# Gate tiles of three head pairs as seven block products, in a float32 encoder step on one core

## What is computed

```python
u = rmsnorm(x, norm_w) @ w_in
cq = rmsnorm(u[..., :Q_LORA_RANK], q_norm_w)
gate = u[..., Q_LORA_RANK:]
q = (cq @ w_uq).reshape(B, T, MLA_HEADS, QK_NOPE_DIM + QK_ROPE_DIM)
q_nope = q[..., :QK_NOPE_DIM]
q_pe = rope(q[..., QK_NOPE_DIM:], q_pos)
q_lat = jnp.einsum('bthn,rhn->bthr', q_nope, kv_w_uk)
o_lat = mla_attend(q_lat, q_pe, q_pos, c_kv, k_pe, k_pos)
o = jnp.einsum('bthr,rhv->bthv', o_lat, kv_w_uv).reshape(B, T, MLA_GATE_WIDTH)
return x + (o * jax.nn.silu(gate)) @ w_out
```

## Time and profile before

| | us |
|---|---|
| median of 3 runs | 1047.45 (1046.79 to 1049.26) |
| the profiled execution's own time | 1046.36 |
| its span | 1044.6 |
| TensorE busy | 1019.8 (98%) |
| VectorE busy | 503.3 (48%) |
| ScalarE busy | 259.6 (25%) |
| GpSimd busy | 271.1 (26%) |

### The profile page before, as it was taken

One profiled execution on the slowest core, in us unless ns is written; L12 is line 12 of the kernel. 1 busy time (PEld: TensorE's weight loads), 2 busy tenths in 40 slices (PEclk: granted clock), 3 DMA queues, 4 the chain that ended last, 5 costly groups with the idle time before them and its releaser, 6 DMA issues.

```text
span 1044.6 us, 12018 instructions
## 1 busy us (share of the span) xinstructions
PE 1019.8 (98%) x4334; PEld 654.8 (63%) x4334; DVE 503.3 (48%) x1134; ACT 259.6 (25%) x541; POOL 271.1 (26%) x345
## 2 busy tenths in 40 slices
PE   7999999999989999999999999999999999999998
PEld 4777777777755453444535777777766666655665
DVE  5964444444466566685665532244233333344224
ACT  3222121212154242232431000011222323243221
POOL 3552525252313234142132063311110101010110
PEclk9999999999999999999999999999999999999999
DMA  7224232423375989979798322112210111203202
GB/s 269 78 99 157 92 109 112 156 90 110 111 298 179 397 323 346 373 302 391 300 374 332 146 81 81 55 46 104 92 64 20 63 41 44 88 31 127 79 27 101
DMA packets 44464, 164.20 MB, mean 157 GB/s; under 512 B 4916, under 2 KB 8248, under 8 KB 35456
## 3 DMA queue, kind: packets, MB, share of 16 engines
q1 hardware_dynamic: 44416, 163.56, 42.5%
HBM read 106.32 MB, written 57.23 MB: 157 GB/s over the span
## 4 chain that ended last, share of the span: by engine, by line
PE 63%; DVE 4%; DMA 1%; POOL 1%; ACT 1%; issue 1%; SPq 0%; POOLq 0%; ACTq 0%
PE work_b L708 11%; PE work_a L708 7%; PE work_b L1246 5%; PE work_a L1037 5%; PE bank L1121 5%; PE work_a L936 3%; PE bank L1004 2%; PE work_b L1121 2%; PE work_b L989 2%; DVE arena L2149 2%; PE bank L1291 2%; PE work_a L1316 2%; PE work_a L1276 1%; PE bank L1425 1%; PE work_a L1121 1%; PE work_a L1013 1%
## 5 line engine op out<-in xcount | busy, mean ns | idle before, releaser
L2149 DVE SCALAR_TENSOR_TENSOR arena<-arena,bank 128x512 f32<-128x512 f32 x128 | 87.0, 742 | 59.3 <-PE bank L1004 59.3
L708 PE MATMUL work_b<-arena,ring 128*128 128x320 f32 x384 | 107.8, 433 | 0.0
L708 PEld LDWEIGHTS work_b<-arena,ring 128*128 128x128 f32 x384 | 71.5, 190 | 27.7
L1037 PE MATMUL work_a<-arena 128*128 128x512 f32 x128 | 64.1, 613 | 2.7 <-ACT arena L1581 2.7
L813 PE MATMUL work_a<-arena 128*128 128x320 f32 x224 | 64.9, 433 | 0.4 <-DVE arena L1916 0.4
L813 PE MATMUL work_a<-arena,ring 128*128 128x320 f32 x224 | 64.9, 432 | 0.0
L813 PE MATMUL work_b<-arena 128*128 128x320 f32 x224 | 62.7, 432 | 0.0
L708 PE MATMUL work_a<-arena,ring 128*128 128x320 f32 x192 | 55.4, 449 | 7.2 <-DMA ring<-in_stream 7.2
L2659 POOL COPY arena<-arena 32x640 f32<-32x640 f32 x20 | 16.6, 832 | 163.0 <-ACT arena L1696 156.7
L813 PEld LDWEIGHTS work_b<-arena 128*128 128x128 f32 x224 | 42.6, 190 | 17.7
L708 PEld LDWEIGHTS work_a<-arena,ring 128*128 128x128 f32 x192 | 37.9, 198 | 23.2 <-DMA ring<-in_stream 7.2
(11 more groups left out here) (336 smaller groups left out, 1795.0 us busy)
## 6 DMA issues: line engine op xcount, KB each, us to landing
ring<-in_stream SPq DMA_DIRECT2D x66, 512.0 KB, 3.4
arena<-in_c SPq DMA_DIRECT2D x32, 1024.0 KB, 9.3
out_s_c<-arena SPq DMA_DIRECT2D x32, 1024.0 KB, 6.1
arena<-in_keys SPq DMA_DIRECT2D x8, 664.0 KB, 4.2
v_scratch<-arena SPq DMA_DIRECT2D x16, 320.0 KB, 4.3
k_scratch<-arena SPq DMA_DIRECT2D x16, 320.0 KB, 4.6
z_scratch<-arena SPq DMA_DIRECT2D x16, 320.0 KB, 4.3
arena<-k_scratch SPq DMA_DIRECT2D x4, 1280.0 KB, 13.0
```

What stands on the lines that cost most here:

```text
L708: done = mm(halves(buf)[:, a, :], lhs, rhs[:, a * HALF:(a + 1) * HALF], start=first, stop=last)
L1037: last = mm(pair_bank[q % 2], kh[:, q, t, :], vh[:, :, t, :], start=t == 0, stop=t == NP - 1)
L2149: op = v.scalar_tensor_tensor(ct[s % CS][:, g, :], ct[s % CS][:, g, :], decb[:, h, b:b + 1], bank[g][:, :], ALU.mult, ALU.add)
```

## The change

The two gate tiles that pairs 0 to 2 prepare are formed together. Their product is taken as 2x2 blocks: rows = the two gate tiles, columns = the left and right 320 tokens, inner dimension = input tiles 0 to 3 (upper) and 4 to 7 (lower). Seven products of four matmuls each (320 columns) replace eight such products. For this
- GpSimd forms four combinations of the tokens (4 tiles x 320 = 1280 columns) once, before pair 0 (`mix_gate_tokens`), and four combinations of the weights (4 blocks x 128 = 512 columns) in each of pairs 0 to 2, after `swap_halves` (`mix_gate_weights`);
- TensorE's `gate_products` issues the products in an order in which two accumulate onto earlier ones in PSUM; the filler portions are 8, 6, 4, 6, 2, 2 matmuls, counted in matmuls now and not in blocks;
- ScalarE's `keep_gate` copies two halves of 320 columns instead of two tiles of 640, after the exponentials of blocks 0 and 1;
- VectorE adds five times 320 columns: `gate_sums` after the probabilities of blocks 0, 2 and 3 (one, one, two), `last_gate_sum` after the pair's outputs;
- SyncE reloads both slots of the ring once all seven products of the pair are through; before, each as its tile was through.

```diff
@@ buffers of the attention stage
+        gate_w_mix = [take(KH, P) for _ in range(2)]
+        gate_u4 = take(HALF)
...
+        spare = [osT.rearrange("p a b c d -> p (a b c d)"), lsq.rearrange("p a b -> p (a b)")]
+        gate_x_mix = [shaped(part[:, 0:KH * HALF], (KH, HALF)) for part in (*spare, keys_c, arena[:, root_at:root_at + 2 * T])]
+        gate_w_mix += [shaped(part[:, KH * HALF:KH * HALF + KH * P], (KH, P)) for part in spare]
+        gate_p1, gate_u2 = rstd[:, 0:HALF], rstd[:, HALF:T]
...
+        GATE_MM, GATE_OUT, GATE_KEPT = 7, 5, 2
+        KEPT_E, MIXED_E = NI - 2 + OUT_PAIRS - 1, MIXED_A + 4 * (OUT_PAIRS - 1)
+        X_MIXED = MIXED_E + 4
@@ SyncE
+                sp.wait_ge(gate_mm, GATE_MM * (p + 1))
                 for r in range(2):
-                    load_weight(at + 8 + 2 * p + r, (2 * p + r) % SLOTS, gate_mm)
+                    load_weight(at + 8 + 2 * p + r, (2 * p + r) % SLOTS, None)
@@ TensorE, stage_e
-                def gate_tiles(k_all):
-
-                    for at in k_all:
-                        r, k = divmod(at, KD)
-                        slot = (2 * p + r) % SLOTS
-                        if k == 0:
-                            pe.wait_ge(w_in[slot], c.next(w_in[slot], step=16))
-                            if r == 0:
-                                pe.wait_ge(E.free[1], c.all(E.free[1]))
-                            else:
-                                pe.wait_ge(gate_out, c.all(gate_out))
-                        last = tokens(work[1], ring[:, slot, k, :], xb[:, k, :], k == 0, k == KD - 1)
-                        if k == KD - 1:
-                            last.then_inc(gate_mm, c.up(gate_mm))
-                            c.skip(gate_out)
-
-                gates = iter(range(2 * KD))
+                def gate_products():
+
+                    s0, s1 = 2 * p % SLOTS, (2 * p + 1) % SLOTS
+                    left, right = slice(0, HALF), slice(HALF, T)
+                    low, high = quarter[2], quarter[3]
+                    out, kept, mixed = GATE_OUT * p, KEPT_E + GATE_KEPT * p, X_MIXED + 4 * p
+
+                    def product(dst, weights, tokens_of, fresh):
+                        for k in range(KH):
+                            last = mm(dst, weights[:, k, :], tokens_of[:, k, :], start=fresh and k == 0, stop=k == KH - 1,
+                                      skip_group_check=True)
+                            if k == KH - 1:
+                                last.then_inc(gate_mm, 1)
+                            yield
+
+                    pe.wait_ge(w_in[s0], c.next(w_in[s0], step=16))
+                    pe.wait_ge(E.free[1], c.all(E.free[1]))
+                    yield from product(low, ring[:, s0, upper, :], xb[:, upper, left], True)
+                    pe.wait_ge(pool_mixed, mixed + 2)
+                    yield from product(high, gate_w_mix[1], gate_x_mix[1], True)
+                    pe.wait_ge(prod_kept, kept + 1)
+                    yield from product(low, ring[:, s0, lower, :], xb[:, lower, left], False)
+                    pe.wait_ge(gate_out, out + 1)
+                    yield from product(high, gate_w_mix[0], gate_x_mix[0], True)
+                    pe.wait_ge(pool_mixed, mixed + 4)
+                    pe.wait_ge(prod_kept, kept + 2)
+                    yield from product(low, gate_w_mix[3], xb[:, lower, right], True)
+                    pe.wait_ge(gate_out, out + 2)
+                    yield from product(high, gate_w_mix[2], gate_x_mix[2], True)
+                    pe.wait_ge(gate_out, out + 4)
+                    pe.wait_ge(w_in[s1], c.next(w_in[s1], step=16))
+                    yield from product(high, ring[:, s1, lower, :], gate_x_mix[3], False)
+
+                gates = gate_products()
 
                 def filler(n_gate, n_out):
 
                     if p < PAIRS - 1:
-                        gate_tiles([next(gates) for _ in range(n_gate)])
+                        for _ in range(n_gate):
+                            next(gates)
                     else:
                         out_calls(n_out)
 
                 scores(0)
-                filler(4, 3)
+                filler(8, 3)
                 scores(1)
                 turn(0)
-                filler(4, 3)
+                filler(6, 3)
                 scores(2)
                 turn(1)
-                filler(2, 2)
+                filler(4, 2)
                 scores(3)
                 turn(2)
-                filler(4, 4)
+                filler(6, 4)
                 turn(3)
                 if p == PAIRS - 1:
                     sample_scores(0)
-                filler(1, 0)
+                filler(2, 0)
                 outputs(0)
                 outputs(1)
-                filler(1, 0)
+                filler(2, 0)
@@ ScalarE, stage_e
+                    act.wait_ge(gate_out, GATE_OUT * p)
+                    act.wait_ge(prod_kept, KEPT_E + GATE_KEPT * p)
...
-                def keep_gate(r):
+                def keep_gate(n):
                     if p == PAIRS - 1:
                         return
-                    act.wait_ge(gate_mm, c.next(gate_mm))
-                    op = nc.scalar.activation(two(gate[:, 2 * p + 2 + r, :]), halves(work[1]), ACT.Copy)
-                    op.then_inc(gate_out, c.up(gate_out))
+                    act.wait_ge(gate_mm, GATE_MM * p + (3 if n else 1))
+                    if n == 0 and p:
+                        act.wait_ge(gate_out, GATE_OUT * p)
+                    dst = gate[:, 2 * p + 2, 0:HALF] if n else gate_p1
+                    nc.scalar.activation(dst, quarter[2], ACT.Copy).then_inc(prod_kept, 1)
...
                 for t in range(NP):
-                    if t == 2:
-                        keep_gate(0)
                     if t:
                         turned(t - 1)
                     for a in range(2):
                         exponentials(E, a, pexp[a][:, 0:(t + 1) * P], (t + 1) * P)
+                    if t < 2:
+                        keep_gate(t)
                     if p == PAIRS - 1 and t >= 2:
                         sample_queries(t - 2)
                 turned(NP - 1)
-                keep_gate(1)
@@ VectorE, stage_e
+                top_gate, low_gate = gate[:, min(2 * p + 2, KD - 2), :], gate[:, min(2 * p + 3, KD - 1), :]
+
+                def add_gate(done, out, part, u):
+                    dve.wait_ge(gate_mm, GATE_MM * p + done)
+                    v.tensor_tensor(out, part, u, ALU.add).then_inc(gate_out, 1)
+
+                def gate_sums(t):
+                    if t == 0:
+                        dve.wait_ge(prod_kept, KEPT_E + GATE_KEPT * p + 1)
+                        add_gate(2, gate_u2, quarter[3], gate_p1)
+                    if t == 2:
+                        dve.wait_ge(gate_out, GATE_OUT * p + 1)
+                        add_gate(4, gate_u4, quarter[3], gate_u2)
+                    if t == 3:
+                        dve.wait_ge(gate_out, GATE_OUT * p + 2)
+                        add_gate(5, top_gate[:, HALF:T], quarter[2], gate_u4)
+                        add_gate(6, low_gate[:, HALF:T], quarter[3], gate_u4)
+
+                def last_gate_sum():
+                    add_gate(7, low_gate[:, 0:HALF], quarter[3], gate_u2)
...
                         probabilities(E, a, pexp[a][:, 0:n])
+                    if p < PAIRS - 1:
+                        gate_sums(t)
...
                 outputs(1)
+                if p < PAIRS - 1:
+                    last_gate_sum()
@@ GpSimd
+            def mix_gate_tokens():
+                pool.wait_ge(normed, 3 * KD)
+                left, right = slice(0, HALF), slice(HALF, T)
+                top_x, low_x = xb[:, 0:KH], xb[:, KH:KD]
+                for n, (a, b) in enumerate(((top_x[:, :, right], top_x[:, :, left]), (low_x[:, :, right], gate_x_mix[0]),
+                                            (low_x[:, :, right], top_x[:, :, right]), (low_x[:, :, left], gate_x_mix[1]))):
+                    if n in (1, 3):
+                        pool.wait_ge(pool_mixed, MIXED_E + n)
+                        pool.wait_ge(latents_ready, 1 if n == 1 else 2)
+                    g.tensor_tensor(gate_x_mix[n], a, b, ALU.subtract).then_inc(pool_mixed, 1)
+
+            def mix_gate_weights(p):
+                w0, w1 = ring[:, 2 * p % SLOTS], ring[:, (2 * p + 1) % SLOTS]
+                if p:
+                    pool.wait_ge(gate_mm, GATE_MM * p)
+                done = X_MIXED + 4 * p
+                for s in (2 * p % SLOTS, (2 * p + 1) % SLOTS):
+                    pool.wait_ge(w_in[s], 16 * (NI // 2 + 7 + (p == 2)))
+                g.tensor_tensor(gate_w_mix[0], w1[:, 0:KH], w1[:, KH:KD], ALU.add).then_inc(pool_mixed, 1)
+                pool.wait_ge(pool_mixed, done + 1)
+                g.tensor_tensor(gate_w_mix[1], gate_w_mix[0], w0[:, 0:KH], ALU.subtract).then_inc(pool_mixed, 1)
+                g.tensor_tensor(gate_w_mix[2], w0[:, 0:KH], w1[:, 0:KH], ALU.subtract).then_inc(pool_mixed, 1)
```

(17 more changed lines are left out.)

## The result

The changed kernel takes 1041.91 us in the median of 8 runs (1039.73 to 1043.86) against 1046.43 us of the kernel before in 8 runs beside them: ratio 0.995 (0.9934 to 0.9966), 4.5 us less. 1043.8 was predicted, 3.6 us less than the median shown then. The profiled execution takes 1039.92 us and spans 1038.1.

A forecast was written before the change was run, and what follows sets the result against it. The prediction took TensorE to bound the changed head pairs: -6.46 for matmuls, +2.55 for held VectorE instructions, +0.3 before the seventh product, -3.6 us, thus 1043.8 us as median, range 1040.8 to 1046.8.

The forecast's parts named there:

- The matmuls saved: TensorE's gate products: 28 matmuls instead of 32 in each of three pairs, 6.46 us off.
- VectorE's instructions held by GpSimd's: Rope of each pair: sum and small copies wait for weight combinations, key copy late, TensorE loses 0.85 us, 2.55 in all.
- no hold: Rival, rope: small copies not stopped, or their hold ends early enough; -6.2 us, 1041.3 us; chance 0.20.
- GpSimd first: Rival, rope: GpSimd's combination starts before VectorE's product, 2.1 us lost per pair; +0.2, 1047.7 us; chance 0.13.
- GpSimd keeps the port: Rival, rope: four queued combinations block VectorE until the last ends, 2.65 us per pair; +1.8, 1049.3 us; chance 0.07.
- The seventh product: After the fourth block, TensorE waits for VectorE's two additions: 0.1 us per pair, bounds 0 and 0.5.
- The cover: Less filler hiding softmax waits: 1.08 us less at two places, no wait; before the last turning 0.8 and 0.3 left.
- ScalarE, the reloads, the tokens: Smaller ScalarE copies, later weight-slot reloads and token mixing before the first pair: each taken as 0.
- The sum: Whole kernel: matmuls, held instructions and seventh-product wait together give -3.6 us.
- the likeliest case's own: Range given for the median if the forecast case holds (chance 0.56): 1042.8 to 1045.0 us.

The follow-up runs named there:

- d1: Changed kernel with no token or weight combinations, the seven products reading plain blocks and tiles: second pair 47.24 us, median 1040.81 us, 0.9945 of the kernel before.
- c1: Changed kernel with GpSimd's weight combinations begun only after VectorE has copied both heads' keys: second pair 47.24 us, median 1040.64 us, 0.9953 of the kernel before.
- c3: Kernel before, gate tiles unchanged, with GpSimd's four weight combinations added unused in pairs 0 to 2: second pair 50.00 us, median 1049.45 us, 1.0025 of the kernel before.
- d4: c1 with one more unused 320-column VectorE addition ahead of the two after block 3: second pair 47.59 us, median 1041.18 us, 0.9954 of the kernel before.
- c0: Changed kernel run again without edit: second pair 47.85 us, median 1042.22 us, 0.9968 of the kernel before.
- e1: c1 run again, on a chip shared with the changed kernel: second pair 47.23 us, median 1039.91 us, 0.9929 of the kernel before.
- c2: Changed kernel with each weight combination made in two halves of 256 columns, same place: second pair 47.24 us, median 1041.63 us, 0.9952 of the kernel before.
- d2: Changed kernel with the weight combinations ahead of the pair's rope copies: second pair 47.24 us, median 1040.04 us, 0.9942 of the kernel before.
- d3: c1 with two filler matmuls moved from before the last turning to the pair's end: second pair 47.76 us, median 1041.01 us, 0.9952 of the kernel before.
- e2: Changed kernel run again without edit, beside e1: second pair 47.84 us, median 1042.42 us, 0.9945 of the kernel before.

## Why the prediction held, and where it was off

- **The matmuls saved**: 6.46 us predicted, 3 x 2.16 = 6.5 measured (d1, c1). Right.
- **VectorE's instructions held by GpSimd's**: right in kind, place and order. VectorE first by hundredths, the sum 1.77 us (1.8 predicted), the small copies 2.41 (2.5), the key copy's end at 13.67 us of the pair (13.72). c3 shows it without the products, c1 takes it away with the products kept. Of the rivals, no hold and GpSimd first are both out; that GpSimd keeps the port is out by the alternation. What was mis-sized is TensorE's loss behind it: 0.60 us (47.84 - 47.24), not 0.85. I had put 0.2 us between the key copy's end and the first matmul, from the spacing of load and matmul in the earlier trace rows. That spacing belongs to a TensorE that still has matmuls to run. With TensorE idle, load and matmul both start 0.05 us behind the copy (819.86). That explains 0.15 of the 0.25 us; another 0.05 is the copy's end, 0.05 us sooner in the pair than predicted, and for the last 0.05 no line shows a cause. In all 0.75 us of the difference.
- **The seventh product**: 0.1 us a pair predicted, 0 measured. The two additions start before the factor ahead of them has ended (846.26 against 846.35) and take 0.91 us together, so they end at 847.17, 0.07 us ahead of the load at 847.24; d4 shows that only 0.03 of it is room. 0.3 us of the difference.
- **The cover**: no wait at the last turning, as predicted, with 0.4 us left for the second head (0.3 predicted; from 846.35 to the fifth load at about 846.75). Nothing at the other turnings.
- **ScalarE, the reloads, the tokens**: nothing, as taken. The reciprocal beside the token combinations kept its 4.15 us; none of the three reloads appears among the waits.
- **The sum**: -3.6 predicted, -4.7 by the rest of the span, -4.5 by the medians. The difference of about 1.1 us is the two terms above.
- **The median**: it alone would not have told the forecast from its rival. 1041.91 lies nearer to the 1041.3 of "no hold" than to 1043.8, and below the 1042.8 to 1045.0 given as the likeliest case's own. Of the 1.9 us, 1.0 is the kernel before, which came out at 1046.43 in 8 runs and not at 1047.45; counted from there the forecast is 1042.8 and no hold 1040.2. What decides is the wait of TensorE, three times, and the held instructions.

The Trainium skill (SBUF — State Buffer, section Who interferes with whom) counts plain copies in SBUF among the instructions that can take the port pair shared with GpSimd. The trace agrees: the two 64x128 copies, 0.22 us each alone, took 1.17 and 1.21 beside GpSimd's combinations of 1.27 us.

## What to carry to other kernels

Work moved to an idle GpSimd is not free by itself. In these runs it cost nothing beside VectorE's copies out of PSUM and beside its reciprocal, and it held sums of two SBUF tiles and float32 copies from SBUF to SBUF. Look up which VectorE instructions run in that stretch, count about one whole GpSimd instruction as the wait of each of the second kind, and follow them to the engine on the path. If they lead there, start the GpSimd work at another point, or cut its instructions shorter. And when the price of a wait of TensorE is a few tenths of a us, count it from the end of the matmuls in flight to the release, not from the weight load.

## What the runs showed beyond that

The scatter of the whole comes from ahead of the attention stage. In the twelve profiled executions the first pair starts between 758.2 and 762.5 us, whatever the kernel, while the rest of the span repeats to 0.1 us for one kernel.

TensorE's clock looks like the cause, and in the main is not. In the execution before and then the one after, 302 to 312 and 310 to 340 us (TensorE, loads, VectorE, ScalarE, GpSimd, granted clock, DMA):

```profile
302.00:312.00 10.00, 7.81 (x33) 4.67 (x32) 7.67 (x14) 7.03 (x12) 0.00 (x0) 1.00 0.99 406
310.00:340.00 30.00, 29.43 (x146) 15.61 (x145) 19.89 (x64) 12.56 (x27) 8.29 (x14) 0.94 0.57 208
```

```profile
302.00:312.00 10.00, 8.67 (x34) 5.20 (x34) 8.11 (x17) 5.42 (x11) 0.00 (x0) 1.00 1.00 405
310.00:340.00 30.00, 28.24 (x143) 14.29 (x142) 20.52 (x64) 11.28 (x24) 9.69 (x18) 1.00 0.59 217
```

The granted clock of 0.94 is one stretch of 3.4 us at the lower level, 1.2 GHz, and 1.00 is none. TensorE had been waiting in part just before, for ScalarE, in both (7.81 and 8.67 of 10 us busy). Of the other profiled executions, four had no such stretch (c0, d1, d4, e1), five had one of 3.4 us (c1, c2, c3, d2, d3), and one had 6.8 us (e2). Half of 3.4 is 1.7 us, close to the 1.8 by which the first pairs' starts differ, but the same instructions on either side of the stretch show that this is chance. The execution before is already 1.66 us behind where TensorE goes on from its first 32 records (18.56 against 16.90 us), 1.67 at GpSimd's combination of the earlier trace rows (106.30 against 104.63) and 1.67 at TensorE's matmul behind the wait for ScalarE (304.32 against 302.65). Behind the stretch it is 1.97 (chain, before and after):

```profile
331.67 2.77 PE work_a L1013 x6
```

```profile
329.70 2.77 PE work_a L1025 x6
```

So the slower matmuls cost 0.3 us in the end. The execution after, faster there, then waits longer for GpSimd (line L920 before, L932 after):

```profile
PE work_b L920 <- POOL arena L2594: 0.5, 1, 0.5
```

```profile
PE work_b L932 <- POOL arena L2651: 1.8, 3, 0.8
```

From that combination (106.30 before) to that matmul (331.67 before) the five executions without a stretch take 225.07 to 225.10 us, the six with 3.4 us 224.74 to 225.37, and e2 228.17: only its 6.8 us cost something, 3.1. The larger differences come with the start of the launch (the combination lies between 104.09 and 106.86) and between that matmul and the first pair (427.7 to 430.5 us); what sets them is open. So kernels whose spans differ by less than about 4 us are better compared from the stage that was changed.
